# Three token norms: a product with an identity that carries the factors, in place of scaled copies and transposes

## The reference

```
def rmsnorm(x, g):
    xf = x.astype(jnp.float32)
    y = xf * lax.rsqrt(jnp.mean(xf * xf, axis=-1, keepdims=True) + NORM_EPS)
    return (y * g.astype(jnp.float32)).astype(x.dtype)

# first block
h = rms_norm(x, mix_norm_g[l])
proj = h @ w_l
...
x = x + jnp.concatenate([out_a, out_b, out_m], axis=-1) @ w_out[l]
x = x + conv_ffn(rms_norm(x, ffn_norm_g[l]), w_up[l], conv_w[l], conv_b[l], w_down[l])

# second block
h = rmsnorm(x, norm1_g[l]) * (1.0 + sc1[:, None, :]) + sh1[:, None, :]
proj = h @ w_in[l]
...
y_ffn = hierarchical_moe(h2, ...)   # 32 experts, their weights read one after the other
```

## Time and profile before

| | |
|---|---|
| median of 3 runs | 1064.72 us (1063.16 to 1065.44) |
| the profiled execution | 1063.16 us, of which the span from first to last instruction is 1061.4 us |
| TensorE | 911.6 us busy (86%), 8462 products recorded |
| weight loads on TensorE | 706.2 us (67%) |
| VectorE | 551.6 us (52%) |
| ScalarE | 358.2 us (34%) |
| GpSimd | 76.0 us (7%) |
| DMA | 316.21 MB, mean 298 GB/s |

### The profile page before, as it was taken

The page is one execution under the profiler, slowest core; times in us unless marked ns, Lnnn a source line. Parts: engine busy times, 40 slices in busy tenths (PEclk is TensorE's granted clock), DMA queues, the critical chain, the costliest instruction groups (busy, mean ns, idle before and its releaser), DMA issues.

```text
span 1061.4 us, 19424 instructions
## 1 busy us (share of the span) xinstructions
PE 911.6 (86%) x8462; PEld 706.2 (67%) x8462; DVE 551.6 (52%) x1020; ACT 358.2 (34%) x698; POOL 76.0 (7%) x113
## 2 busy tenths in 40 slices
PE   9999999999999999999999998667655666657784
PEld 8787777489999888988989965334333343334442
DVE  4775688858888766798867643211112121211211
ACT  5710355246776536456553341000001010000002
POOL 3022710000000000331010000000000000000000
PEclk9999999999999999999999999988888887989878
DMA  9545453695554565876549899999999999999994
GB/s 350 164 165 185 143 190 120 219 286 170 160 174 174 202 233 190 267 233 215 179 148 387 350 386 426 430 427 430 426 431 427 429 428 429 430 427 429 426 431 200
DMA packets 76715, 316.21 MB, mean 298 GB/s; under 512 B 4087, under 2 KB 28064, under 8 KB 64208
## 3 DMA queue, kind: packets, MB, share of 16 engines
q1 hardware_dynamic: 71972, 302.24, 72.5%
q0 software_dynamic: 4512, 12.62, 4.0%
q10 hardware_dynamic: 140, 0.04, 0.0%
HBM read 311.72 MB, written 1.06 MB: 295 GB/s over the span
## 4 chain that ended last, share of the span: by engine, by line
PE 61%; DMA 25%; DVE 7%; ACT 3%; issue 3%; ACTq 0%; SPq 0%; POOL 0%; DVEq 0%
PE ps L486 59%; DMA w<-in_w_up 18%; DMA w<-in_w_down 4%; DMA w<-in_w_gate 3%; DVE sp L1940 1%; DMA rot<-q 1%; PE ps L612 1%; PE ps L2803 1%; DVE acc L1003 0%; ACT hts L2937 0%; DVE wr L680 0%; DVE w L1041 0%; ACTq L3200 0%; ACT sp L1931 0%; DVE q L2314 0%
## 5 line engine op out<-in xcount | busy, mean ns | idle before, releaser
L486 PE MATMUL ps<-w,xg 128*32 128x256 f32 x2016 | 156.5, 469 | 96.7 <-DMA w<-in_w_up 75.8
L486 PE MATMUL ps<-hb,sp 128*128 128x256 f32 x1824 | 224.4, 283 | 0.0
L486 PEld LDWEIGHTS ps<-hb,sp 128*128 128x128 f32 x1824 | 218.6, 188 | 3.0 <-issue 2.5
L486 PEld LDWEIGHTS ps<-w,xg 128*32 128x32 f32 x2016 | 83.3, 130 | 167.5 <-issue 143.6
L1940 DVE TENSOR_TENSOR sp<-w,sp 128x1024 fp32r<-128x1024 f32 x122 | 144.6, 1220 | 37.5 <-ACT sp L1931 37.4
L1931 ACT ACTIVATE sp<-w 128x1024 fp32r<-128x1024 f32 x122 | 122.3, 1052 | 46.0 <-PE ps L486 42.4
L3013 DVE TENSOR_TENSOR cst<-ps,cst 64x256 f32<-64x256 f32 x31 | 13.3, 428 | 214.6 <-ACT cst L2924 214.6
L2924 ACT ACTIVATE cst<-ps 64x256 f32<-64x256 f32 x31 | 11.7, 377 | 309.8 <-PE ps L486 309.8
L3039 DVE TENSOR_TENSOR ost<-ps,cst 32x256 f32<-32x256 f32 x120 | 50.5, 420 | 103.3 <-PE ps L486 100.5
L486 PE MATMUL ps<-w,hts 128*32 128x256 f32 x1024 | 63.6, 390 | 13.1 <-ACT hts L2937 10.3
L486 PE MATMUL ps<-sp,ab 128*128 128x512 f32 x264 | 61.7, 395 | 0.0
(11 more groups left out here) (430 smaller groups left out, 1304.7 us busy)
## 6 DMA issues: line engine op xcount, KB each, us to landing
w<-in_w_down SPq DMA_DIRECT2D x36, 2048.0 KB, 35.8
w<-in_w_gate SPq DMA_DIRECT2D x32, 2048.0 KB, 28.1
w<-in_w_up SPq DMA_DIRECT2D x31, 2048.0 KB, 33.1
w<-in_w_in SPq DMA_DIRECT2D x13, 2048.0 KB, 9.5
w<-in_w_up SPq DMA_DIRECT2D x22, 1024.0 KB, 7.6
w<-in_w_ada SPq DMA_DIRECT2D x8, 2048.0 KB, 8.7
w<-in_w_out SPq DMA_DIRECT2D x4, 2048.0 KB, 8.0
w<-in_w_ada POOLq DMA_DIRECT2D x8, 768.0 KB, 5.8
```

The costliest lines, as they stand in the source:

```text
L486: return q.eng.matmul(o, l, r, start=start, stop=stop, skip_group_check=True)
```

## The change

The scaled copy goes for norms 0, 2 and 3. In its place ScalarE writes, right behind the root, a 128 by 128 matrix `dg`: the identity with each row times its token's factor. TensorE then turns `x` itself, with an ordinary fp32 product of each block with `dg`, which scales it on the way. `feat_pe` for these norms waits for ScalarE's semaphore instead of VectorE's. Norm 1 keeps its copies and transposes. Two more things change for norm 3: the turn of the first half moves from behind part 4 of the down projection's second half into the middle of its last part (after two of its four k), and a root of a constant ahead of the squares brings ScalarE's table load forward.

```
+        def diag_sc(q, n, h):
+            q.eng.activation(diag[n][:, 128 * h:128 * h + 128], ident, ACT.Copy, scale=nss[:, 2 * n + h:2 * n + h + 1]).then_inc(s["nsc"], 1)
...
         def roots_sc(q, n):
...
                 e.activation(nss[:, 2 * n + h:2 * n + h + 1], nrr[:, 2 * n + h:2 * n + h + 1], ACT.Sqrt).then_inc(s["nsc"], 1)
+                if n == 0:
+                    q.wait_ge(s["cst"], 16)
+                    q.wait_ge(s["nsc"], 2 * h + 3)
+                    diag_sc(q, n, h)
...
         def later_root_sc(q, n):
...
+            q.wait_ge(s["nsc"], NSC[n] + 5)
+            diag_sc(q, n, 1)
-
-        def later_norm_ve(q, n, src, dst):
+
+        def later_norm_ve(q, n):
...
-            q.wait_ge(s["nsc"], 4 * n + 4)
-            for z in range(2):
-                sl = slice(512 * z, 512 * z + 512)
-                e.tensor_scalar(v(dst, 2)[:, 1, sl], src[:, 1, sl], a, None, MUL).then_inc(s["nve"], 1)
...
         def feat_pe(q, n, src, freed, hs=(0, 1)):
...
-                        t = q.eng.transpose(psum[b][:, 128 * i:128 * i + 128], v(src, 2)[:, h, 128 * (k + i):128 * (k + i) + 128], ident)
+                        o, a = psum[b][:, 128 * i:128 * i + 128], src[:, h, 128 * (k + i):128 * (k + i) + 128]
+                        if n == 1:
+                            t = q.eng.transpose(o, a, ident)
+                        else:
+                            t = mm(q, o, a, diag[n][:, 128 * h:128 * h + 128])
...
-            def part(c, h, z):
+            def part(c, h, z, inside=None):
...
+                    if k == 2 and inside:
+                        inside()
...
-                    t = part(4, h, z)
+                    t = part(4, h, z, between if h and z else None)
                     if h:
                         t.then_inc(s["half_mm"], 1)
-                if h:
-                    between()
...
             down_sc(q)
+            q.eng.activation(sml(111, 1), ones[:, 0:1], ACT.Sqrt)
...
             norms_ve(q, 0)
-            scaled_ve(q, 0, x, Xn)
```

More of the change, by code:

```diff
@@ L250, in block_kernel @@
         Ub = [sb(f"ub{i}", 49328 + 1024 * i, 1024) for i in range(2)]
-        xn2 = sb("xn2", 47264, 2048)
+        diag = {n: sb(f"dg{n}", o, 256) for n, o in ((0, P1 + 6288), (2, RB + 8192), (3, 47264))}
         ht2 = sb("ht2", 49312, 2048)
@@ L536, in scaled_ve @@
             for h in range(2):
-                q.wait_ge(s["nsc"], 4 * n + h + 3)
+                q.wait_ge(s["nsc"], NSC[n] + h + 3)
                 e.tensor_scalar(v(dst, 2)[:, h, :], src[:, h, :], nss[:, 2 * n + h:2 * n + h + 1], None, MUL).then_inc(s["nve"], 1)
         def nve_of(n, h):
-            return 6 * n + 3 * h + (n > 2) + (n > 3)
+            return NVE[n] + (3 if n == 4 else 2) * h
         def norm_sc(q, n, src, rdy, junk, hs=(0, 1)):
@@ L548, in norm_sc @@
                     q.wait_ge(*w)
-                q.wait_ge(s["nsc"], 4 * n + 2 * h)
+                q.wait_ge(s["nsc"], NSC[n] + (2 if n == 4 else 3) * h)
                 e.activation(junk, src[:, h, :], ACT.Square, accum_out=nss[:, 2 * n + h:2 * n + h + 1]).then_inc(s["nsc"], 1)
@@ L552, in norm_sc @@
                 e.activation(nss[:, 2 * n + h:2 * n + h + 1], nrr[:, 2 * n + h:2 * n + h + 1], ACT.Sqrt).then_inc(s["nsc"], 1)
+                if n < 4:
+                    q.wait_ge(s["nsc"], NSC[n] + 2)
+                    diag_sc(q, n, h)
         part_ss = sml(144, 4)
         def later_squares_sc(q, n, src, rdy, junk):
-            q.wait_ge(s["nsc"], 4 * n + 2)
+            q.wait_ge(s["nsc"], NSC[n] + 3)
             for z, sums in enumerate((part_ss[:, n:n + 1], nss[:, 2 * n + 1:2 * n + 2])):
@@ L573, in later_norm_ve, with first_norm_ve @@
             e.reciprocal(b, b).then_inc(s["nve"], 1)
-            q.wait_ge(s["nsc"], 4 * n + 4)
-            for z in range(2):
-                sl = slice(512 * z, 512 * z + 512)
-                e.tensor_scalar(v(dst, 2)[:, 1, sl], src[:, 1, sl], a, None, MUL).then_inc(s["nve"], 1)
         def by_k(a):
             return a.rearrange("p (n k) -> p k n", k=8)
-        def norm_ve(q, n, src, dst, after=(), hs=(0, 1), order=None):
+        def first_norm_ve(q, n):
             e = q.eng
[L585 to L597, removed]
+            a, b = nss[:, 2 * n:2 * n + 1], nrr[:, 2 * n:2 * n + 1]
+            q.wait_ge(s["nsc"], NSC[n] + 1)
+            e.tensor_scalar(b, a, 1.0 / 1024, 1e-6, MUL, ADD).then_inc(s["nve"], 1)
+            q.wait_ge(s["nve"], nve_of(n, 0) + 1)
+            e.reciprocal(b, b).then_inc(s["nve"], 1)
         FB = [(0, 1, 2, 3), (4, 5, 6, 7), (0, 1, 2, 3), (0, 1, 4, 5), (0, 1, 2, 3)]
@@ L604, in feat_pe @@
                 for k in range(0, 8, 4):
-                    if n < 2:
-                        q.wait_ge(s["nve"], 6 * n + 5 + h)
+                    if n == 1:
+                        q.wait_ge(s["nve"], NVE[1] + 5 + h)
                     else:
-                        q.wait_ge(s["nve"], nve_of(n, h) + 3 + (k // 4 if h else 0))
+                        q.wait_ge(s["nsc"], NSC[n] + (4 + 2 * h if n == 0 else 3 + 3 * h))
                     b = FB[n][2 * h + k // 4]
@@ L3320, in _ @@
                 wout_ve(q, 0, (i - 6,))
-            norm_ve(q, 2, x, xn1, hs=(0,))
+            first_norm_ve(q, 2)
             split_ve(q, 0)
@@ L3333, in _ @@
             xffn_ve(q, 0)
-            norm_ve(q, 3, x, xn2, hs=(0,))
+            first_norm_ve(q, 3)
             split_ve(q, 33)
@@ L3338, in _ @@
             split_ve(q, 34, (0,))
-            later_norm_ve(q, 3, x, xn2)
+            later_norm_ve(q, 3)
             split_ve(q, 34, (1,))
@@ L3446, in _ @@
                 if n == 1:
-                    feat_pe(q, 2, xn1, ft2, hs=(0,))
+                    feat_pe(q, 2, x, ft2, hs=(0,))
             take(q, 6)
```

42 lines of the change are left out of this document (21 added, 21 removed).

## The result

| | before | after |
|---|---|---|
| median of 7 runs each, on the same chip | 1063.20 us (1061.88 to 1065.49) | 1067.87 us (1065.25 to 1071.43) |
| ratio of the runs, after to before | | 1.0047, 95% interval 1.0031 to 1.0062 |
| the profiled execution | 1063.16 us, span 1061.4 | 1065.25 us, span 1063.5 |

The changed kernel is slower by 0.47% by the ratio of the runs, and its median lies 4.67 us higher; the forecast was 1069.0 us, from 4.8 us of loss, in a range of 1064.5 to 1071.0. The two profiled executions lie only 2.1 us apart, less than half of that. So the stages are read first, and what hides the rest of the loss in these two traces comes behind them.

The account below looks back on a forecast made before the run. TensorE was taken to bound up to 447 us and the experts' weights from 620 us. Losses of 1.1 + 1.1 + 0.9 + 0.5 + 1.2 = 4.8 us at the norms gave 1069.0 us, range 1064.5 to 1071.0.

Parts of the forecast that it names:

- TensorE bounds at the norms: Up to 447 us TensorE limits the kernel; delays at the three norms reach the end one for one.
- The price of a half: Turning half a norm's tokens by fp32 products: 1.98 us on TensorE in place of 0.87 or so.
- Norm 0: +1.1: TensorE starts 0.54 us earlier, but slower pieces delay its first three-part product by 1.1 us.
- Norm 2: +1.1 and +0.9: TensorE pays 1.1 us more for the first half's turn and 0.9 net for the second.
- Norm 3: +0.5 and +1.2: First half 0.5 us later, ScalarE's split waiting behind the moved turn; second half 1.2 later from its longer turn.
- The sum: 4.8 us: Total loss over norms 0, 2 and 3: 1.1 + 1.1 + 0.9 + 0.5 + 1.2.
- The forecast's starting time: The profiled 1063.16 us was taken as the lowest of three runs, 1.56 below their median.
- Absorbed ahead of the experts: Rival: DMA's 7.3 us of room between 557 and 620 us makes up the late front; 1064.7 to 1066.8 us, chance 0.18.
- the 4 to 5 us that the prediction gave as its sign: Sign of a right forecast: the stream of the experts' weights comes 4 to 5 us later.
- As cheap as a transpose: Rival: products at the norms turn as fast as transposes, leaving 1.4 us of gains; 1063.3 us, chance 0.12.
- Four records: Rival: each product at the norms takes four records, not two; 16.7 us lost, 1081 us, chance 0.03.
- Not what it says: Rival: the change fails, say ScalarE's table load returns behind `dg`; under 1.3 us, mostly covered, no change; chance 0.02.

Follow-up runs that it names:

- norm 0 alone: The kernel before with only norm 0 changed to matrices and products, the rest as before: 1065.02 us (before 1062.70), ratio 1.0027.
- the kernel with plain transposes: The changed kernel with its scaling products taken back to transposes of the tokens, factors left out, all else as changed: 1061.95 us, one run.

## Why the prediction was right

**TensorE bounds at the norms, and its added time passes to the end.** Right at the norms, and right for the end as far as the timed runs can tell. Issuing the transposes twice, which adds TensorE time and nothing else, gives 1.0032 (1.0011 to 1.0053), beside the change's 1.0047 (1.0031 to 1.0062); taking the product's price away turns the loss at the norms (0.87, 1.84 and 1.05 us) into gains (0.47, 0.11 and 0.42). So the product costs some 4.8 us in the trace, and the rest of the change gives 1.0 back.

**The price of a half.** Right in kind, two records for each product, and 5 to 16% too high: 1.98 us were taken, and measured are 1.79 and 1.89 (norm 2), 1.70 and 1.70 (norm 3), and 3.67 for both halves of norm 0. This is the mis-sized term, and it runs through all steps. The Trainium skill (TensorE: Matmul & The Clock Gate, section Terms) puts the transpose mode at 4 times the speed for fp32; the trace differs, with 1.79 against 0.87 us for the same half, 2.1 times. The prediction's own bound, that no row shows a ratio above 2.3, overlooked norm 3: 1.98 against its 0.80 is 2.5.

**Norm 0: +1.1, measured +0.87.** VectorE loses eight instructions over the three norms (1020 to 1012 on the page) and not five as written; no term rests on it. The places are the ones named: the root at 8.49, the first `ht` at 10.50 (10.44 forecast), the fourth at 13.11 (13.41), the three-part product at 17.39 (17.6). A start 0.10 later than forecast (9.23 for 9.13) and 3.67 us for the two halves in place of 3.96 make the difference.

**Norm 2: +1.1 and +0.9, measured 0.91 and 0.93 (second trace 0.91 and 0.86).** Right: no new wait arose.

**Norm 3: +0.5 and +1.2, measured 0.23 and 0.82 (second trace 0.27 and 0.81).** The split was late behind the moved turn as argued (it waits 2.51 us for TensorE), and putting the turn back recovers the 0.27. The sizes come out at half and two thirds, the half costing 1.70 and not 1.98.

**The sum: 4.8 us.** The three norms make 3.8 us. What the sum lacks is a term that it did not know: the second stop of TensorE near 135 us, which makes 0.2 to 0.7 us. With it the front comes to some 4.0 to 4.5 us, against 4.67 between the medians. The second traces of both kernels, free of the first ones' troubles, agree: 3.07 us apart at 432 us, 4.2 with the 1.1 us that the trace of the kernel before lost to its clock near 184 us. The terms too large and the term that was missing partly cancelled, so that 4.8 lies so near 4.67 is in part luck. The forecast's starting time was some 1.0 us too high: it took the profiled 1063.16 us for a low run, and over seven runs the median is 1063.20.

**Absorbed ahead of the experts (0.18).** Against it stand the medians: the change's interval is 3.3 to 6.6 us, and norm 0 alone, 1.57 us late at 432 us, still costs 0.27% (0.10 to 0.44). The prediction named what decides: whether the first loads of the experts are issued later. They are. SyncE's first one in the two traces of the kernel before, then in the two of the kernel after:

```profile
553.04 0.34 SPq L3186 DMA_DIRECT2D w<-in_w_gate  x1
```

```profile
552.01 0.34 SPq L3186 DMA_DIRECT2D w<-in_w_gate  x1
```

```profile
555.62 0.34 SPq L3190 DMA_DIRECT2D w<-in_w_gate  x1
```

```profile
554.09 0.34 SPq L3190 DMA_DIRECT2D w<-in_w_gate  x1
```

In all the traces of the table the loads from there to 608 us are later (or earlier) by what it has at 553 us, to within 0.03 us: up to there nothing is made up in the stretch that this rival named. But the loads are 2.6 us later (2.1 between the second traces), and not the 4 to 5 us that the prediction gave as its sign. Part of the front's lateness is gone between 432 and 465 us. There VectorE needs the `rot<-q` transfers, which GpSimd issues; in five of the ten traces it waits for them (0.26 to 3.25 us). The issue of the last one ahead of 465 us is as late as the table's 432 in every trace but the second of before, but its time to landing varies from 2.8 to 9.2 us. The change from 432 to 465 us is -0.6 us on average in the five traces that lose 0.87 us or more in norm 0 and -0.9 in the five others, so it does not favour the late ones. Behind 553 us single executions move by -0.9 to +2.1 us against the trace of before, up to 1050 us; norm 0 alone, 1.57 us late at 432, is 0.04 late there. Whether a small part is made up there can't be told from ten traces; that most of it is not is what the timed runs say.

**As cheap as a transpose (0.12)** would have given gains near those of the kernel with plain transposes, 1.0 us at the norms (1.4 forecast), and rows of 16 records in 1.7 us or more rule it out. **Four records (0.03):** 96 records for 48 products rule it out. **Not what it says (0.02):** the table is loaded ahead of norm 3, and the matrix takes 0.40 us right behind the root.

## What to carry to other kernels

Before work is moved to the engine that bounds a stage, price it there in records: an fp32 product with a scaled identity is two where a transpose is one, and the instructions that it saves elsewhere become waiting for it. Doubling the suspected work in the old kernel, and undoing only that work in the new one, shows from both sides whether it is the cause. Before two traces are subtracted, take a second one of each program, and count only the steps that come back. More instructions on an engine can also cost time where nothing was edited: here a second stop of TensorE, 120 us further on, came in every trace with 16 records more in norm 0 and in no other.

## What was not expected of the hardware

Single stretches at the lower clock come and go between executions of one program: the granted clock of 0.66 and 0.83 at 57 to 64 us cost one execution 1.7 us, after a wait of TensorE of 0.48 us that executions without it have too. Five of the ten traces have this stretch (0.76 over 57 to 64 us), the other five 1.00, and the two of one program differ.

TensorE's stops near 135 and 142 us, put down to "issue", stand ahead of its 1237th product in every trace, and ahead of its 1110th in those with 16 records more in norm 0, 1.4 to 1.6 us behind the end of a 16 KB transfer of the "instruction" queue.

In the first trace of the kernel after, and in no other, the products of `hb` with `sp` stood 120.0 ns apart in place of 118.7, which made 1.4 us from 231 to 400 us (1.51 to 2.87 in the table).
